# Triangular inverses of the gated delta rule: from six doubling levels on the matrix engine to 32x32 blocks solved by columns on the vector engine, with two levels left on the matrix engine

## The chip, the cores and the metric

The kernel runs on one core of a Trainium2 chip. The metric is the device time of one execution, in microseconds. Its engines are TensorE (PE in the profile; its weight loads are PEld), VectorE (DVE), ScalarE (ACT), GpSimd (POOL) and SyncE (SP, which only issues weight DMAs here).

## The reference, cut to what matters

Two transformer blocks on 256 tokens of width 2048: an attention block with a Fourier block, then a token mixer (a delta-rule part beside dilated attention) and a gated MLP. The change is in the delta-rule part of the token mixer, which has 8 heads of 128 and runs once forwards and once backwards over the tokens:

```python
def gated_delta_chunked(q, k, v, g, beta):
    ...
    cum_g = jnp.cumsum(g, axis=-1)
    gamma = jnp.exp(jnp.where(lower, cum_g[..., :, None] - cum_g[..., None, :], NEG_INF))
    k_beta = k * beta[..., None]
    a_mat = jnp.where(strict, jnp.einsum("bhnik,bhnjk->bhnij", k_beta, k) * gamma, 0.0)
    t_mat = a_mat + jnp.eye(c, dtype=jnp.float32)
    u = triangular_solve(t_mat, v * beta[..., None])
    w = triangular_solve(t_mat, k_beta * jnp.exp(cum_g)[..., None])
    qk = jnp.einsum("bhnik,bhnjk->bhnij", q, k) * gamma
    ...
    def step(state, xs):                      # over the chunks
        v_new = u_n - w_n @ state
        o_n = qd_n @ state + qk_n @ v_new
        state = state * dec_n + kt_n.T @ v_new
# q, k, v: silu of a depthwise convolution of width 5 over the projection n @ w_in; q, k normalized by head
o = delta(q, k, v, g_f, beta_f) + flip(delta(flip(q), flip(k), flip(v), flip(g_b), flip(beta_b)))
o = rms_norm(o) * silu(z)                     # then @ w_out, with the dilated half
```

## The kernel before, in words

The order of instructions on each engine is written out by hand. Weight matrices come in units of 128x2048 words (1 MB), which SP loads into four slots of `raw`. ACT copies a unit, rounded, into one of three `high` buffers (`act_hi`), DVE subtracts to get the rest (`dve_lo`), and PE runs three products a tile (high by high, high by low, low by high): 48 products of 128x256 a unit. ACT and DVE work two units ahead; `act_hi` of unit u waits until PE has used unit u - 3. Eight linears of four units make the inputs of the delta part: `("qkv", 0..5)` (q in 0 and 1, k in 2 and 3, v in 4 and 5) and `("z", 0..1)`. Beside them, as a `side` generator that is advanced once a unit, DVE runs the convolution (`dve_conv`, 24 tiles of 128x256, five operations each), and ACT the silu.

Then comes the delta part by itself (`pe_delta`, `dve_delta`, `act_delta`, end of `gpsimd_program`), and no linear runs beside it. The 256 tokens are two chunks of 128, so there are 16 matrices of 128x128 a direction (8 heads x 2 chunks), handled as 4 groups n of 4 matrices; one operation of 128x512 covers a group. In order: norms of q and k (`head_rstd`, `apply`), then for each direction `dr`: the decay matrices G from rows that PE spreads with a product by ones, A = beta * (k k^T) * G, the products k q, and the inverse of I + A by doubling. X starts as the inverse of 2x2 blocks, and level l = 1 to 6 joins pairs of blocks: POOL masks A by a constant (`L`), PE forms Y = L X, ACT copies Y, PE forms dXT and dX, DVE subtracts both. Then the scan over the two chunks (`vn` new values, `S` state, `kS`, `o` output), and after both directions the norm of the sum, the product with z, and its split into high and low. Only then does the next linear (`oM`, by `w_out`) start.

All products of the delta part are in plain float32; a product of 128 columns has two records in the trace, a transpose one.

## Time and profile before

| | us |
|---|---|
| median of 3 runs | 3241.22 (3228.16 to 3261.13) |
| the profiled execution, its time | 3227.28 |
| its span | 3225.5 |
| PE busy in the span | 3071.2 (95%) |
| DVE busy | 1855.3 (58%) |
| ACT busy | 1271.4 (39%) |
| POOL busy | 246.3 (8%) |

The first columns say what the whole takes. The page's 40 slices of the span (80.6 us each) show where: DMA falls from 192 GB/s to 33, 1 and 1 GB/s in slices 27 to 29, which is the delta part, where no weights are needed and the four slots are full.

### The profile page before, as it was taken

How to read it: one execution, taken by the hardware profiler on the slowest of the kernel's cores; microseconds unless marked ns; L12 is line 12 of the kernel's file. 1: busy time of each engine (PE TensorE's matmuls, PEld its weight loads, DVE VectorE, ACT ScalarE, POOL GpSimd, SP SyncE). 2: the span in 40 equal slices, each digit the busy share in tenths (PEclk: the TensorE clock that was granted, in tenths of full speed). 3: DMA queues.
4: the chain of work that ended last, by engine and by line, in shares of the span. 5: the costliest groups of instructions: out<-in, count | busy, mean ns of one | idle time of the engine just before them, and what ended most of it. 6: DMA issues, size and time to landing. Idle time of an engine off the chain costs nothing.

```text
span 3225.5 us, 52600 instructions
## 1 busy us (share of the span) xinstructions
PE 3071.2 (95%) x23262; PEld 2822.2 (87%) x23262; DVE 1855.3 (58%) x2132; ACT 1271.4 (39%) x1326; POOL 246.3 (8%) x244
## 2 busy tenths in 40 slices
PE   6999989988999999999999999998979999999998
PEld 3699775588988998989999989978879999999998
DVE  6746765466766434464544537755445667456653
ACT  7723331134433344343433425432233444344444
POOL 0001001000000000002112110032400000000000
PEclk8999999998999999989999989989989999999999
DMA  8746545354665553435444435500024555555553
GB/s 346 301 167 232 213 149 182 128 202 149 250 228 203 194 196 140 150 132 173 157 158 157 149 107 195 192 33 1 1 78 153 191 195 190 196 199 192 192 191 135
DMA packets 90850, 548.04 MB, mean 170 GB/s; under 512 B 10592, under 2 KB 10624, under 8 KB 45568
## 3 DMA queue, kind: packets, MB, share of 16 engines
q1 hardware_dynamic: 69408, 465.86, 40.4%
q0 software_dynamic: 18432, 67.12, 5.8%
q10 hardware_dynamic: 2784, 11.70, 0.9%
q8 instruction: 184, 3.01, 0.4%
q14 instruction: 42, 0.34, 0.0%
HBM read 542.54 MB, written 2.10 MB: 169 GB/s over the span
## 4 chain that ended last, share of the span: by engine, by line
PE 88%; DVE 5%; ACT 2%; issue 2%; DMA 1%; SPq 0%; DVEq 0%; ACTq 0%
PE bank L663 87%; DVE r L1812 2%; ACT r L1242 1%; DMA f<-in_units 1%; PE bank L725 1%; PE bank L994 0%; DVE f L1865 0%; DVE f L2351 0%; DVE f L2121 0%; ACT f L1359 0%; DVE f L1846 0%; DVE f L2240 0%; DMA f<-in_later 0%; DVE f L1988 0%; DVE f L2138 0%
## 5 line engine op out<-in xcount | busy, mean ns | idle before, releaser
L663 PE MATMUL bank<-r,r 128*128 128x256 f32 (+4 forms) x19360 | 2409.2, 287 | 62.3 <-DVE r L1812 31.3
L663 PEld LDWEIGHTS bank<-r,r 128*128 128x128 f32 (+3 forms) x19360 | 2297.4, 188 | 166.8 <-issue 76.3
L1812 DVE TENSOR_TENSOR r<-f,r 128x2048 fp32r<-128x2048 f32 (+2 forms) x466 | 1012.6, 2175 | 853.3 <-ACT r L1242 851.5
L1242 ACT CAST r<-f 128x2048 fp32r<-128x2048 f32 (+2 forms) x466 | 835.6, 1796 | 985.2 <-PE bank L663 803.3
L663 PE MATMUL bank<-f,f 128*128 128x128 f32 (+12 forms) x3390 | 639.4, 338 | 50.2 <-issue 7.3
L663 PEld LDWEIGHTS bank<-f,f 128*128 128x128 f32 (+6 forms) x3390 | 472.1, 196 | 161.5 <-issue 88.0
L1846 DVE SCALAR_TENSOR_TENSOR f<-f,f,f 128x512 f32<-128x512 f32 x240 | 180.0, 750 | 40.0 <-DMA f<-in_later 32.4
L2540 POOL DMA_DIRECT2D f<-in_later x128 | 67.8, 529 | 968.2 <-DVE f L1846 790.4
L1259 ACT COPY f<-bank 128x512 f32<-128x512 f32 (+2 forms) x141 | 80.2, 588 | 148.0 <-PE bank L663 142.5
L2289 DVE SCALAR_TENSOR_TENSOR f<-f,f,f 128x255 f32<-128x255 f32 (+1 forms) x272 | 131.7, 484 | 9.7
L2549 POOL TENSOR_TENSOR f<-f,f 32x512 f32<-32x512 f32 x24 | 30.9, 1289 | 735.5 <-PE bank L663 735.5
L725 PEld LDWEIGHTS bank<-f,f 128*128 128x128 f32 x288 | 37.4, 159 | 52.5 <-issue 20.3
L1408 ACT ACTIVATE f<-bank,f 128x512 f32<-128x512 f32 x32 | 22.0, 688 | 150.3 <-DVE f L1995 143.8
L2567 POOL TENSOR_TENSOR f<-f,f 128x512 f32<-128x512 f32 x56 | 72.2, 1313 | 52.3 <-PE bank L663 47.4
L2357 DVE TENSOR_TENSOR f<-f,bank 128x512 f32<-128x512 f32 x48 | 33.0, 688 | 69.2 <-PE bank L663 69.2
L725 PE MATMUL bank<-f,f 128*128 128x128 f32 x288 | 48.8, 310 | 25.1 <-ACT f L1408 10.1
L2552 POOL TENSOR_TENSOR f<-f,f 32x512 f32<-32x512 f32 x24 | 64.4, 2683 | 1.9
L1593 ACT COPY f<-bank 128x512 f32<-128x512 f32 x48 | 28.1, 586 | 87.5 <-PE bank L663 87.5
L1988 DVE TENSOR_REDUCE f<-bank 128x1 f32<-128x512 f32 x32 | 22.0, 689 | 57.2 <-PE bank L663 57.2
L1522 ACT ACTIVATE f<-f,f 128x768 f32<-128x768 f32 x16 | 15.0, 938 | 80.1 <-DVE f L2248 80.1
L2227 DVE TENSOR_TENSOR f<-bank,f 32x512 f32<-32x512 f32 x24 | 16.3, 679 | 45.4 <-PE bank L663 45.4
L1359 ACT ACTIVATE f<-f 128x256 f32<-128x256 f32 (+1 forms) x46 | 19.1, 433 | 50.8 <-PE bank L663 29.2
(205 smaller groups left out, 898.6 us busy)
## 6 DMA issues: line engine op xcount, KB each, us to landing
f<-in_units SPq DMA_DIRECT2D x346, 1024.0 KB, 4.8
f<-in_units SPq DMA_DIRECT2D x120, 768.0 KB, 4.3
f<-in_later POOLq DMA_DIRECT2D x128, 512.0 KB, 4.9
f<-in_units SPq DMA_DIRECT2D x8, 576.0 KB, 4.7
f<-in_x ACTq DMA_DIRECT2D x2, 1024.0 KB, 12.7
f<-in_ctx ACTq DMA_DIRECT2D x2, 1024.0 KB, 11.3
f<-in_x_turned ACTq DMA_DIRECT2D x1, 2048.0 KB, 11.1
f<-in_units SPq DMA_DIRECT2D x2, 800.0 KB, 4.4
```

Of the source, the lines that this page charges most:

```text
L663: return e.matmul(o, lhsT, rhs, start=start, stop=stop, skip_group_check=True)
L725: ins = e.transpose(o[:, j * 128:(j + 1) * 128], src(j), ident)
L1242: e.copy(unit_view(high[HIGH_OF[u]][1], u), unit_view(raw[RAW_OF[u]][0], u)).then_inc(*up("w_hi", ("hi", u)))
L1259: return e.copy(dst, src(ps("lin", name, q))).then_inc(*up("act_out", ("out", "lin", name, q), *names))
L1812: e.tensor_tensor(unit_view(raw[RAW_OF[u]][1], u), unit_view(raw[RAW_OF[u]][0], u), unit_view(high[HIGH_OF[u]][1], u).bitcast(F32), ALU.su ...
L1846: ins = e.scalar_tensor_tensor(o, w, s, o, ALU.mult, ALU.add)
L2289: ins = e.scalar_tensor_tensor(o[:, lo:hi], s[:, lo + d:hi + d], tap(j), o[:, lo:hi], ALU.mult, ALU.add)
L2357: e.tensor_tensor(gXT[:, n, :], gXT[:, n, :], ps("dXT", dr, l, n)[:, :], ALU.subtract).then_inc(*up("dve_delta", ("out", "dXT", dr, l, n), ...
L2540: e.dma_start(own[:, n % 2, :, :], a["later"][n // 8, n % 8].rearrange("p (k c) -> p k c", k=2)).then_inc(*up(f"own_half{n % 2}", ("own la ...
L2549: e.tensor_tensor(v, v, cos2.unsqueeze(1).to_broadcast([32, 2, T]), ALU.mult).then_inc(*up("pool_dil"))
L2552: e.tensor_tensor(v, v, two(rt[n % 2][0:32, :]), ALU.add).then_inc(*up("pool_dil", ("roped half", x, hf, br), ("half", n)))
L2567: e.tensor_tensor(v4(gL[:, m, :]), v4(gAT[:, m, :]), b4(ec[f"{lev}{l}"]), ALU.mult).then_inc(*up("pool_delta", ("L", dr, l, m)))
```

## The change

- The order of the linears is k, z, q, v (`MIXER`), and part of the delta work is run beside them: `pe_delta_ahead`, `act_delta_ahead` and `dve_delta_ahead`, each advanced once a unit (`under`). The 32 units of the eight linears are counted from 0 to 31 here; the numbers of `yield` set the unit.
- Ahead go the gates, the decay matrices of both directions (now Relu and Exp on ACT, from products that spread one column), the norm of k, k k^T (once for both directions), A (into `TT`, all 32 matrices), and the root of q's norm.
- DVE transposes the 32x32 diagonal blocks of A into `FF`, 32 matrices with four blocks each, and solves all 128 blocks at once by columns: 31 steps, each a product of a column by the rows solved so far and a subtraction, into `VB`. It needs `TT` at unit 18, and runs in units 19 to 24 of 32.
- After the linears `VB` is transposed into the diagonals of `VV` and `UU` (the inverses and their transposes), which lie where the linears' operand H was and are set to zero by POOL when the last two units are done.
- PE runs levels 5 and 6 alone. In level 6 and in half of level 5's products only 64 columns are computed.
- The products of k and q are shared by both directions, whose scans go side by side. Both directions add up in the same PSUM banks.
- Buffers of the delta part lie in the three `high` buffers, so the first units of `oM` are not split beforehand (`upto`). Unit 0 of `oM` is split once the last forward output exists, the others later.
- Five of the 24 convolution tiles are left for the delta part.

```diff
+MIXER = [("qkv", 2), ("qkv", 3), ("z", 0), ("z", 1), ("qkv", 0), ("qkv", 1), ("qkv", 4), ("qkv", 5)]
+TILES = [4 * b + i for name, b in MIXER if name == "qkv" for i in range(4)]
+CONV_RATE = [0, 0, 0, 0] + [1, 1, 1, 1] + [2, 2, 0, 0] + [0] * 12 + [2, 2, 1, 2] + [1, 1, 1, 1]
+GRP = [[(c, hf) for c in order for hf in range(2)] for order in ((0, 1), (1, 0))]
...
+def under(first, rates, second):
+    for n in rates:
+        run_on(first, n)
+        run_on(second)
+        yield
...
+        gL, gY = quads(high[0][0][:, :]), quads(high[1][0][:, :])
+        gG = [quads(high[2][0][:, :]), quads(flat3(TT)[:, 2048:4096])]
...
+            for dr in range(2):
+                for n in range(4):
+                    pe_gate_rows(e, SIDE, "G", dr, n)
+                    if n % 2 == 1:
+                        yield
+            for _ in range(5):
+                yield
+            for _ in pe_head_rstd(e, "dlk", 8, sqk):
+                pass
+            yield
+            yield
+            for p in range(4):
+                pe_apply(e, "dlk", 1, p, (2 * p, 2 * p + 1))
+                if p % 2 == 1:
+                    yield
+            for hf in range(2):
+                for c in range(2):
+                    pe_with_k(e, SIDE, "kk", c, hf, 8)
+                yield
+            for _ in range(13):
+                yield
+            for _ in pe_head_rstd(e, "dlq", 8, sqq):
+                pass
+            yield
...
+        def pe_delta(e):
+            four = range(4)
+            for n in four:
+                pe_gate_rows(e, ALLB, "Gq", 0, n)
+            for p in four:
+                pe_apply(e, "dlq", 0, p, (2 * p, 2 * p + 1))
+            for dr in range(2):
+                for n in four:
+                    pe_level_y(e, 5, dr, n)
+                for n in four:
+                    pe_level_5(e, dr, n)
+                if dr == 0:
+                    for n in (0, 1):
+                        pe_gate_rows(e, ALLB, "Gq", 1, n)
+                else:
+                    pe_turned_k(e, 0)
+                for n in four:
+                    pe_level_y(e, 6, dr, n)
+                for n in four:
+                    pe_level_6(e, dr, n)
+                if dr == 0:
+                    for n in (2, 3):
+                        pe_gate_rows(e, ALLB, "Gq", 1, n)
+            pe_turned_k(e, 1)
+            for c in range(2):
+                for hf in range(2):
+                    pe_with_k(e, ALLB, "kq", c, hf, 0)
...
+            for _ in range(17):
+                yield
+            e.wait_ge(*at("solved"))
+            e.wait_ge(*at("qkv", 7))
+            for _ in act_squares(e, "hrs", "dlq", [qkv[:, i, :] for i in range(8)], sqq, T):
+                pass
+            yield
+            act_head_root(e, "dlq", 0, 1.0)
+            yield
...
+        def act_delta(e, conv):
+            e.wait_ge(*at("used", LIN[MIXER[-1]].us[3]))
+            for n in range(4):
+                act_gate_rows(e, 0, n)
+            act_y(e, 5, 0)
+            act_y(e, 6, 0)
+            for n in range(4):
+                act_gate_rows(e, 1, n)
+            act_y(e, 5, 1)
+            act_y(e, 6, 1)
...
+            dve_head_rstd(e, "dlk", 1)
+            yield
+            for p in range(4):
+                dve_apply(e, "dlk", p, qkv[:, 8 + 2 * p:10 + 2 * p, :], 1.0)
+                if p % 2 == 1:
+                    yield
+            for hf in range(2):
+                for c in range(2):
+                    o = ps("kk", c, hf)
+                    e.wait_ge(*at("ps", "kk", c, hf))
+                    for dr in range(2):
+                        n = GRP[dr].index((c, hf))
+                        e.wait_ge(*at("exp G", dr, n))
+                        for j in range(4):
+                            v, x = mats(TT, dr, n)[:, j, :], 8 * dr + 4 * hf + j
+                            names = [("A", dr, n)] + ([("out", "kk", c, hf)] if dr else []) if j == 3 else []
+                            e.scalar_tensor_tensor(v, o[:, j * 128:(j + 1) * 128], bt[:, c, x:x + 1], v, ALU.mult, ALU.mult).then_inc(
+                                *up("dve_delta", *names))
+                yield
+            e.wait_ge(*now("dve_delta"))
+            for q in range(4):
+                qs_ = slice(32 * q, 32 * q + 32)
+                e.transpose(FF[qs_, :, :], TT[qs_, :, qs_].rearrange("p m a -> p a m")).then_inc(*up("dve_delta", ("F laid",)))
+            yield
+            e.wait_ge(*at("eye"))
+            for b in range(31):
+                k = 31 - b
+                t = tmpS[:, 0:k * (b + 1)].rearrange("p (a c) -> p a c", a=k)
+                w = VB[:, b + 1:32, 0:b + 1]
+                e.wait_ge(*now("dve_delta"))
+                e.tensor_tensor(t, FF[:, b + 1:32, b].unsqueeze(2).to_broadcast([128, k, b + 1]),
+                                VB[:, b, 0:b + 1].unsqueeze(1).to_broadcast([128, k, b + 1]), ALU.mult).then_inc(*up("dve_delta"))
+                e.wait_ge(*now("dve_delta"))
+                e.tensor_tensor(w, w, t, ALU.subtract).then_inc(*up("dve_delta", ("solved",)))
+                if b % 6 == 5 or b == 30:
+                    yield
+        def dve_turned_back(e):
+            e.wait_ge(*at("zero"))
+            e.wait_ge(*at("solved"))
+            for q in range(4):
+                qs_ = slice(32 * q, 32 * q + 32)
+                e.transpose(VV[qs_, :, qs_].rearrange("p m c -> p c m"), VB[qs_, :, :].rearrange("p a c -> p c a")).then_inc(
+                    *up("dve_delta", ("V laid",)))
+            yield
+            for q in range(4):
+                qs_ = slice(32 * q, 32 * q + 32)
+                e.transpose(UU[qs_, :, qs_].rearrange("p m a -> p a m"), VB[qs_, :, :]).then_inc(*up("dve_delta", ("U laid",)))
+            yield
...
+        def dve_delta(e, conv):
+            dve_head_rstd(e, "dlq", 0)
+            back = dve_turned_back(e)
+            run_on(back)
+            for p in range(4):
+                dve_apply(e, "dlq", p, qkv[:, 2 * p:2 * p + 2, :], B_SCALE)
+            run_on(back)
+            run_on(conv)
             for dr in range(2):
+                dve_qdec(e, dr)
+                dve_level_5(e, dr)
+                if dr == 1:
+                    dve_ktail(e, 0)
+                run_on(conv)
+                dve_level_6(e, dr)
+                run_on(conv)
+            dve_ktail(e, 1)
...
+            side = under(conv, CONV_RATE, dve_delta_ahead(e))
+            for name in MIXER:
+                dve_units(e, name, side, upto=first_unit(("oM", 0)) - 1)
+            dve_delta(e, conv)
...
+            us = LIN[MIXER[-1]].us
+            for u, m0, m1 in ((us[2], 0, 24), (us[3], 24, 32)):
+                e.wait_ge(*at("used", u))
+                e.memset(VV[:, m0:m1, :], 0.0).then_inc(*up("pool_delta"))
+                e.memset(UU[:, m0:m1, :], 0.0).then_inc(*up("pool_delta", ("zero",)))
             for dr in range(2):
+                for n in range(4):
+                    if dr == 1:
+                        e.wait_ge(*at("ps", "Y", 5, 0, n))
+                    e.wait_ge(*at("A", dr, n))
+                    e.tensor_tensor(v4(gL[:, n, :]), mats(TT, dr, n), b4(ec["pairs"]), ALU.mult).then_inc(*up("pool_delta", ("L", dr, n)))
+                e.wait_ge(*now("pool_delta"))
+                e.wait_ge(*at("F laid"))
+                e.memset(TT[:, 16 * (1 - dr):16 * (2 - dr), 0:64], 0.0).then_inc(*up("pool_delta", ("low zero", dr)))
```

What stands on DVE beside the linears, before (one unit of the convolution's stretch; L1812 is the subtraction of a unit, L2281 and L2289 the convolution of one tile):

```order
L1812 TENSOR_TENSOR r_2048_54<-f_2048_53,r_2048_58 128x2048
L2281 TENSOR_SCALAR f_6144_237<-f_2048_239,f_637_65 128x256
L2289 SCALAR_TENSOR_TENSOR f_6144_237<-f_2048_239,f_637_65,f_6144_237 128x254
L2289 SCALAR_TENSOR_TENSOR f_6144_237<-f_2048_239,f_637_65,f_6144_237 128x255 x2
L2289 SCALAR_TENSOR_TENSOR f_6144_237<-f_2048_239,f_637_65,f_6144_237 128x254
L1812 TENSOR_TENSOR r_2048_56<-f_2048_55,r_2048_62 128x2048
```

And after, units 16 to 19 (L1993 is the subtraction of a unit now, L2517 makes A, L2531 and L2534 are one column step of the solve):

```order
L1993 TENSOR_TENSOR r_2048_50<-f_2048_49,r_2048_58 128x2048
L2517 SCALAR_TENSOR_TENSOR f_4096_241<-bank,f_32_107,f_4096_241 128x128 x16
L1993 TENSOR_TENSOR r_2048_52<-f_2048_51,r_2048_60 128x2048
L2517 SCALAR_TENSOR_TENSOR f_4096_241<-bank,f_32_107,f_4096_241 128x128 x16
L1993 TENSOR_TENSOR r_2048_54<-f_2048_53,r_2048_62 128x2048
L2523 STREAM_TRANSPOSE f_1024_251<-f_4096_241 32x1024 x4
L1993 TENSOR_TENSOR r_2048_56<-f_2048_55,r_2048_58 128x2048
L2531 TENSOR_TENSOR f_256_253<-f_1024_251,f_1024_252 128x31
L2534 TENSOR_TENSOR f_1024_252<-f_1024_252,f_256_253 128x31
L2531 TENSOR_TENSOR f_256_253<-f_1024_251,f_1024_252 128x60
L2534 TENSOR_TENSOR f_1024_252<-f_1024_252,f_256_253 128x30x2
```

Work on A and the solve has moved in between the subtractions that PE's weights wait for. On PE, where the linears have ended, before (L725 transposes; f_2048_247 to 241 are A, L and X):

```order
L663 MATMUL bank<-f_768_91,f_1475_63 128x256 x16
L663 MATMUL bank<-f_32_105,f_2048_233 128x8
L725 MATMUL bank<-f_1475_63,f_6144_237 128x128 x16
L663 MATMUL bank<-f_2048_243,f_1475_63 128x512 x4
L663 MATMUL bank<-f_2048_249,f_1475_63 128x512 x4
L663 MATMUL bank<-f_6144_237 128x128 x32
L725 MATMUL bank<-f_1475_63,f_2048_245 128x128 x16
L663 MATMUL bank<-f_2048_241,f_2048_249 128x128 x16
L663 MATMUL bank<-f_2048_245,f_2048_243 128x128 x4
L663 MATMUL bank<-f_2048_243,f_2048_245 128x128 x4
```

and after (f_4096_117 is `VV`, f_4096_119 `UU`, f_2048_57 the masked A, f_2048_59 the copy of Y, f_4096_241 `TT`):

```order
L697 MATMUL bank<-f_384_233,f_32_105 128x128 x16
L697 MATMUL bank<-f_768_91,f_1475_63 128x256 x8
L697 MATMUL bank<-f_4096_117,f_2048_57 128x128 x16
L697 MATMUL bank<-f_2048_59,f_4096_119 128x64 x4
L697 MATMUL bank<-f_4096_119,f_2048_59 128x128 x4
L697 MATMUL bank<-f_384_233,f_32_105 128x128 x8
L697 MATMUL bank<-f_4096_117,f_4096_241 128x64 x16
L697 MATMUL bank<-f_4096_119,f_2048_59 64x64 x16
```

The six levels are gone from this place, and levels 5 and 6 of the forward direction follow the norm of q directly.

## Rows read from the trace of the kernel before

**Rows 1.** The page, part 4: who holds the chain that ended last, whole span.

```profile
PE 88%; DVE 5%; ACT 2%; issue 2%; DMA 1%; SPq 0%; DVEq 0%; ACTq 0%
```

**Rows 2.** Windows: from:to, length, busy (count) of each engine, PE clock, DMA share, GB/s.

```profile
1930.00:2104.40 174.40, 174.40 (x1530) 174.21 (x1528) 127.02 (x158) 80.48 (x79) 0.00 (x0) 0.99 0.55 193
2104.40:2155.10 50.70, 43.90 (x193) 29.66 (x193) 32.31 (x46) 18.25 (x36) 14.95 (x11) 0.83 0.06 21
2155.10:2215.90 60.80, 60.80 (x547) 60.80 (x546) 27.77 (x43) 14.65 (x25) 26.50 (x22) 1.00 0.01 1
2215.90:2267.40 51.50, 37.70 (x219) 31.35 (x217) 30.60 (x45) 11.10 (x19) 15.39 (x11) 0.86 0.00 0
2267.40:2329.40 62.00, 62.00 (x545) 62.00 (x545) 27.76 (x43) 14.62 (x25) 26.17 (x22) 0.98 0.01 1
2329.40:2359.00 29.60, 19.52 (x122) 17.92 (x120) 9.07 (x16) 3.51 (x6) 0.00 (x0) 0.83 0.00 1
2359.00:2379.60 20.60, 9.85 (x33) 5.00 (x33) 10.93 (x16) 11.26 (x19) 0.00 (x0) 0.74 0.00 0
2104.40:2379.60 275.20, 233.78 (x1650) 206.72 (x1649) 138.43 (x207) 73.39 (x130) 83.02 (x64) 0.90 0.01 5
```

**Rows 3.** Timeline of PE in the delta part: start, length, engine, line, operation, shape, count.

```profile
2118.71 11.22 PE L663 MATMUL bank<-f,f 8*128 8x256 f32 x36 [0.18 <-DVE f L1941]
...
2155.11 60.91 PE L663 MATMUL bank<-f,f 128*128 128x128 f32 x544
...
2241.98 10.92 PE L663 MATMUL bank<-f,f 128*128 128x128 f32 x32 [0.72 <-ACT f L1597]
...
2267.36 62.22 PE L663 MATMUL bank<-f,f 128*128 128x128 f32 x544
...
2367.55 5.73 PE L663 MATMUL bank<-f,f 8*128 8x256 f32 x16 [2.95 <-DVE f L1937]
```

**Rows 4.** The same view, small float32 products in an earlier stage.

```profile
705.49 1.84 PE L663 MATMUL bank<-f,f 128*128 128x4 f32 x16
```

**Rows 5.** Timeline of DVE beside the linears, same columns.

```profile
1953.25 0.18 DVE L2267 TENSOR_SCALAR f<-f 128x32 f32<-128x32 f32 x1 [2.16 <-ACT f L1550]
1953.46 0.19 DVE L2269 TENSOR_TENSOR f<-f,f 128x32 f32<-128x32 f32 x1
...
1957.66 2.29 DVE L1812 TENSOR_TENSOR r<-f,r 128x2048 fp32r<-128x2048 f32 x1 [2.20 <-ACT r L1242]
...
1960.25 2.04 DVE L2289 SCALAR_TENSOR_TENSOR f<-f,f,f 128x254 f32<-128x254 f32 x4
```

**Rows 6.** DVE's groups by shape, whole span: count | busy us, mean ns | idle.

```profile
L2357 DVE TENSOR_TENSOR f<-f,bank 128x512 f32<-128x512 f32 x48 | 33.0, 688 | 69.2 <-PE bank L663 69.2
...
L2351 DVE TENSOR_TENSOR f<-f,f 128x512 f32<-128x512 f32 x8 | 9.4, 1236 | 0.0
L1937 DVE RECIPROCAL f<-f 8x256 f32<-8x256 f32 x5 | 8.7, 1740 | 17.9 <-ACT f L1382 17.9
...
L2138 DVE SCALAR_TENSOR_TENSOR f<-f,f,bank 128x256 f32<-128x256 f32 x32 | 14.0, 476 | 2.0 <-PE bank L663 2.0
...
L1918 DVE TENSOR_TENSOR r<-f,r 128x1024 fp32r<-128x1024 f32 x4 | 4.9, 1220 | 0.0
```

**Rows 7.** POOL's groups, whole span.

```profile
L2567 POOL TENSOR_TENSOR f<-f,f 128x512 f32<-128x512 f32 x56 | 72.2, 1313 | 52.3 <-PE bank L663 47.4 <-DVE f L2346 3.6 <-DVE f L2351 1.3
...
L2609 POOL MEMSET const-float32-0.0<- 128x1 f32 x1 | 0.1, 98 | 0.2 <-issue 0.2
```

**Rows 8.** ACT's groups, whole span.

```profile
L1242 ACT CAST r<-f 128x2048 fp32r<-128x2048 f32 x342 | 653.1, 1911 | 760.0 <-PE bank L663 650.8 <-DMA f<-in_units 107.9 <-issue 1.2
...
L1583 ACT ACTIVATE f<-f 128x512 f32<-128x512 f32 x8 | 5.0, 626 | 5.0 <-DVE f L2333 5.0
...
L1539 ACT COPY f<-bank 128x256 f32<-128x256 f32 x8 | 3.0, 373 | 26.4 <-PE bank L663 26.4
```

More of the change, by code:

```diff
@@ L183, in plan @@
     add("ab", w, KT, [(4096, 32)], [(128, 32)] * 2)
-    for b in range(6):
-        add(("qkv", b), w, KT, [(512 * b, 512)], full * 4)
-    for b in range(2):
-        add(("z", b), w, KT, [(3072 + 512 * b, 512)], full * 4)
+    for name, b in MIXER:
+        add((name, b), w, KT, [((3072 if name == "z" else 0) + 512 * b, 512)], full * 4)
     for b in range(4):
@@ L2554, in gpsimd_program @@
                         n += 1
[L2555 to L2568 removed]
+            e.wait_ge(*at("ps", "dtv", 3, 1))
```

631 lines of the change are left out of this document (342 added, 289 removed).

## The prediction

> **What bounds the kernel now.** I read the chain that ended last first: PE holds 88% of it [rows 1], so time comes off only where PE works less or waits less. Then the 40 slices show a stretch without weight transfers, and windows cut it at the events of the timeline [rows 2]. The delta part, from the end of the linears (2104.4) to the first product of `oM` (2379.6), takes 275.2 us, all of it on the path. The reader is to see two kinds of row in it: the levels (60.8 and 62.0 us) with PE busy throughout at full clock, and the rest (50.7, 51.5, 29.6, 20.6) with PE waiting for ACT and DVE, at a granted clock of 0.74 to 0.86. The linears ahead of it (174.4 us for 32 units, 5.44 a unit) have PE full, but DVE busy for only 127.0 and ACT for 80.5. The change takes products from PE and puts work into that room on DVE.
>
> **Prices.** A float32 product of 128 columns costs 60.91 / 272 = 0.224 us [rows 3], at two of the 544 records a product; one by the norm's 256 columns 5.73 / 8 at a mixed clock, 0.45 at full clock (twice 0.224). Of 4 columns it costs 1.84 / 8 = 0.23 us, the same [rows 4]: the 64-column products save no PE time, and I price them at 0.224. The page "TensorE: Matmul & The Clock Gate" of the Trainium skill (Back-to-back issue gap) has an isolated gap of columns / 2.4 GHz + 2.5 ns; by it the 96 half-width products would cost half and the sum would be 10.7 us lower, against the row. A dependent small DVE operation follows the one before after 0.21 us with 32 elements [rows 5], and large ones grow by 1.04 ns an element (2.29 us for 2048, 1.22 for 1024) [rows 5, 6]: 0.2 us + 1.04 ns an element for a step that waits for the one before. A tile of convolution is 2.4 us.
>
> **Beside the linears, PE.** Added: sums of the gates 16 records (1.8), gate rows 32 products (7.2), k's norm 8 of 256 columns (3.6), its spreading 8 of 256 (3.6), k k^T 16 (3.6), q's norm 8 of 256 (3.6): 23.4 us, all on the path, as PE is full there.
>
> **Beside the linears, DVE.** The solve has 62 operations on sum (31-b)(b+1) = 5,456 elements, twice: 62 x 0.2 + 10,912 x 1.04 ns = 12.4 + 11.4 = 23.8 us. A from k k^T is 32 operations of 128 elements from PSUM, 0.33 us each (476 ns for 256 [rows 6], less 128 elements): 10.6. The norm of k takes 1.74 + 4 x 0.69. The four transposes into `FF` show in no row. From below they are bounded by 1024 contiguous elements, 1.22 us, from above by the slowest two-operand row, 1.236 us for 512 [rows 6], so 2.47; both sides of this operation hop in memory or work on strips, so I take the middle, 1.85, 7.4 for four. Off DVE go five tiles (12 us), moved behind the linears. In total 127 + 35 = 162 us of some 198: there is room on average. Locally there is not. Between units 16 and 27 DVE has 12 x 2.21 (subtractions) + 10.6 + 7.4 + 23.8 + 7 tiles (16.8) = 85.1 us, against PE's 12 x 5.44 + 1.8 = 67.1. It is 18 us behind; its lead is two units less the cast and subtraction (10.9 - 1.9 - 2.3 = 6.7 [rows 5, 8]) plus the k k^T beside it, 8.5. The remaining **10 us** are a wait of PE for the low part, in units 23 to 30. Bounds: with 1.22 a transpose 6 us; with 2.41 ns an element throughout (the 1236 ns row) 15 + 2.5 more, 27. Queued behind a late DVE are the convolution's tiles, then ACT's silu and next cast, which have slack of a unit.
>
> The page "Vector Engine (DVE) Microarchitecture Reference" of the Trainium skill (section 5.2) says that a stream which hops at each element costs 1.7 to 2.5 ns for a column in place of 1.05. By it a transpose would be 1.9 to 2.7 us, near or just over my upper end, and the rule speaks against this change; the solve's streams mostly run along rows and would keep the low price. No row of this trace hops, so it cannot say.
>
> **Behind the linears.** T is the end of unit 31.
> (a) To the point where `UU` is laid. POOL clears `VV` and `UU`: 3072 elements each after unit 30, 1024 each after 31. A clearing of one element shows 98 ns, a POOL product of 512 shows 1313, or 2.56 ns an element [rows 7]. It reads nothing, so I take 1 ns, near the 0.93 of ACT's casts [rows 8], which gives T + 3; at 2.56 it is T + 15. Behind that wait stand on DVE the `VV` transposes (7.4), four `apply` (2.8) and the `UU` transposes (7.4): **20.6 us**. PE has only 16 gate rows, 8 spreads and 16 products Y here, 10.8 us, hidden. Range 12.6 to 38.
> (b) From there to the end of level 6 backwards: 160 products (level 5 forwards 32, gate rows 16, Y and last of level 6 forwards 32, Y of level 5 backwards 16, and then 32 + 32), 35.8 us, and 8 transposes 1.0. PE waits for a bank that DVE frees after a convolution tile and a decayed q (2.9), for ACT's two gate groups ahead of its copies of Y (2.1: four Relu of some 0.27, two Exp of 0.6 each [rows 8]) and some 1 elsewhere: **43 us**.
> (c) Scan, both directions at once: DVE's k q products and right sides (1.4 + 8 x 0.61 + 4 x 0.61) end 10 us in, then 48 products (state, o, kS) 10.8, the last right side, new values and copy 3.7, 32 products 7.2: **32 us**. Its two counterparts before are 51.5 with the products ahead of the second direction in it, and 29.6 [rows 2].
> (d) From the last output to `oM`: 20.6 as before [rows 2] and 1.4 for copies: **22 us**. The split of `oM`'s first units hides in the norm and in unit 0.
> (e) Clock. The same 8-column and 8-row products that take 0.22 a record at full clock take 11.22 / 36 = 0.31, and 32 records take 10.92 in place of 3.6 where PE had been waiting [rows 3]. I add **8 us** for (b) and (c).
> Together 125.6 in place of 275.2.
>
> **The sum.** -275.2 + 125.6 + 23.4 + 10 = **-116 us**. The profiled execution's own time is 3227.3, of which 1.8 lies around its span; it becomes 3111. The median shown is 3241.2, 14 above it, and a median is what will be compared: **3125 us**. The rest of the kernel keeps its instructions.
>
> **The rivals.**
> - The vector engine's new work is slow (hops at 2.4 ns an element or more): 17 us more beside the linears, 8 in (a), about 3150. For it: no row shows such an access. Against: only the transposes hop at each element.
> - PE stays at the low clock: (b) and (c) hold 240 products, 54 us; with gaps at half clock they take up to 54 more, some of it inside waits. Rows of the delta part at 0.83 to 0.86 with a third of the time idle [rows 2] speak for about 35 more in all: 3155.
> - Cheaper than thought: transposes at 1.2, no clock loss in (b), PE's waits gone: 3095.
> - Slower than before: the solve paces the linears. 62 dependent operations lie between subtractions, and PE gets no weights while they run. From 0.38 us each (23.8 / 62) they would have to go to about 2.3 for the 116 us to be gone, 2.5 for 3250. The rows give 0.21 for small dependent ones [rows 5], tenfold less. A POOL that holds DVE up (the 1236 ns row stands beside POOL work) has nothing to do there.
> - The change doesn't move the work: the pieces ahead wait for each other and are still unfinished at T. `solved` is needed at unit 30 by q's norm and DVE would have caught up by then; a lag of 20 us would only shift time: 3145.
>
> **How the numbers follow.** Forecast 0.60 (3095 to 3150). Slow vector work 0.15, low clock 0.12, unfinished work 0.04, cheaper 0.07, slower 0.02. Leaving out half of the cheap and the far end of the dear cases, the range is **3085 to 3170**. A measurement of this kernel can tell about 1% (32 us, the spread of the three runs) from no change. All cases but the last are beyond it: faster 0.96, the same 0.02, slower 0.02.
>
> **What would show it.** The profile after should have the first product of `oM` some 116 us earlier; the linears at 205 to 210 us with PE's wait for the low part in units 23 to 30 and nowhere before; solve steps of 0.2 to 0.46 us; transposes between 1.2 and 2.5; a gap of PE after the first 16 Y products, ended by DVE's transposes and not by POOL; 64-column products at 0.22 each. The prediction is wrong if PE waits in units 2 to 15 for the gates or k's norm, if the clearing takes over 5 us, or if `oM`'s first four units run slower than 5.44 us by more than a few.

## The result

The changed kernel takes 3135.3 us (median of 4 runs, 3116.0 to 3144.6) against 3235.1 beside it: 0.967 of the kernel before, 95% interval 0.959 to 0.975. A later set of 6 runs gave 3119.5 us and 0.964 (0.959 to 0.968). The forecast was 3125, within 3085 to 3170. The profiled execution took 3116.0 us with a span of 3114.2; the forecast for it was 3111.

The chain that ended last (page, part 4), to be read beside [rows 1]: DVE has taken over a part of what PE held.

```profile
PE 84%; DVE 9%; ACT 3%; issue 3%; DMA 1%; POOL 0%; SPq 0%; ACTq 0%; DVEq 0%; POOLq 0%
```

The windows that answer to [rows 2], cut at the four steps of the prediction: the linears, then (a) until `UU` is laid, (b) to the end of level 6, (c) to the last output, (d) to `oM`, and the sum of these four.

```profile
1933.90:2152.00 218.10, 207.23 (x1698) 199.84 (x1698) 155.82 (x240) 104.84 (x139) 5.40 (x2) 0.97 0.45 155
2152.00:2175.00 23.00, 14.22 (x87) 12.42 (x85) 19.71 (x14) 11.98 (x29) 18.55 (x16) 0.78 0.14 46
2175.00:2216.00 41.00, 38.51 (x326) 37.64 (x326) 24.66 (x48) 15.63 (x40) 5.07 (x4) 0.92 0.00 1
2216.00:2250.00 34.00, 31.83 (x282) 31.32 (x281) 19.52 (x41) 9.80 (x16) 0.00 (x0) 1.00 0.00 1
2250.00:2271.00 21.00, 9.64 (x32) 4.83 (x33) 10.62 (x16) 14.36 (x23) 0.00 (x0) 0.76 0.00 1
2152.00:2271.00 119.00, 94.20 (x721) 86.20 (x720) 74.51 (x117) 51.77 (x107) 23.61 (x20) 0.89 0.03 10
```

The delta part went from 275.2 to 119.0 us, since PE has 721 records in it instead of 1650. The linears, counted here from the first product of `ab` (a small linear right ahead of unit 0, which the first window above leaves out) to the end of the last unit, went from 191.6 (1912.76 to 2104.4) to 236.0 (1916.05 to 2152.0). Net: -156.2 + 44.4 = -111.8 here, -111.3 in the spans. So less than a third of what the delta part lost came back in the linears; the question was which part of those 44.4 us is work, and which is waiting.

PE's timeline in the linears shows both: pieces of side work (`128x8`, `128*8`, `8*128`), and in brackets what it waited for. `L1993` is DVE's subtraction that makes a unit's low part, `L1486` ACT's squares of q.

```profile
1916.05 30.08 PE L697 MATMUL bank<-r,r 128*128 128x32 f32 x192
1949.10 2.44 PE L697 MATMUL bank<-f,f 128*128 128x8 f32 x16 [2.98 <-issue]
1951.39 8.39 PE L697 MATMUL bank<-r,r 128*128 128x256 f32 x48
1959.62 1.95 PE L697 MATMUL bank<-f,f 128*128 128x128 f32 x16
1961.32 5.90 PE L697 MATMUL bank<-r,r 128*128 128x256 f32 x48
...
2088.87 5.72 PE L697 MATMUL bank<-r,r 128*128 128x256 f32 x48 [0.39 <-DVE r L1993]
2096.43 12.91 PE L697 MATMUL bank<-r,r 128*128 128x256 f32 x96 [1.84 <-DVE r L1993]
2109.51 5.72 PE L697 MATMUL bank<-r,r 128*128 128x256 f32 x48 [0.17 <-DVE r L1993]
2116.72 5.72 PE L697 MATMUL bank<-r,r 128*128 128x256 f32 x48 [1.48 <-DVE r L1993]
2123.60 11.17 PE L697 MATMUL bank<-r,r 128*128 128x256 f32 x96 [1.16 <-DVE r L1993]
2135.03 5.73 PE L697 MATMUL bank<-r,r 128*128 128x256 f32 x48 [0.26 <-DVE r L1993]
2142.76 3.61 PE L697 MATMUL bank<-f,f 128*8 128x256 f32 x16 [2.00 <-ACT f L1486]
```

DVE's timeline at the end of the linears and in (a). The bracket of the first transpose is POOL's clearing; from there to 2174.31 DVE doesn't stop but for PE's last spreading product.

```profile
2139.43 0.35 DVE L2462 TENSOR_SCALAR f<-f,f 128x256 f32<-128x256 f32 x1
2139.81 2.04 DVE L2470 SCALAR_TENSOR_TENSOR f<-f,f,f 128x254 f32<-128x254 f32 x4
2141.77 1.84 DVE L2462 TENSOR_SCALAR f<-f,f 128x256 f32<-128x256 f32 x1
...
2153.97 8.91 DVE L2544 STREAM_TRANSPOSE f<-f 32x1024 f32<-32x1024 f32 x4 [3.89 <-POOL f L2811]
2162.91 1.88 DVE L2122 SCALAR_TENSOR_TENSOR f<-f,bank 128x512 f32<-128x512 f32 x3
2165.82 0.69 DVE L2122 SCALAR_TENSOR_TENSOR f<-f,bank 128x512 f32<-128x512 f32 x1 [1.03 <-PE bank L697]
2166.43 7.88 DVE L2549 STREAM_TRANSPOSE f<-f 32x1024 f32<-32x1024 f32 x4
```

### The profile page after: what moved, and what is told of

Its sections match the earlier page's. It is cut to its first block, busy times and chain, and to the rows that moved or that the text cites. A ratio compares the mean times of both kernels' runs of the same rounds, so it can differ in the third digit from the quotient of the medians.

```text
span 3114.2 us, 50912 instructions
## 1 busy us (share of the span) xinstructions
PE 2963.5 (95%) x22494; PEld 2725.6 (88%) x22494; DVE 1821.7 (58%) x2125; ACT 1273.2 (41%) x1361; POOL 193.5 (6%) x204
## 4 chain that ended last, share of the span: by engine, by line
PE 84%; DVE 9%; ACT 3%; issue 3%; DMA 1%; POOL 0%; SPq 0%; ACTq 0%; DVEq 0%; POOLq 0%
PE bank L697 83%; DVE r L1993 3%; ACT r L1369 1%; DMA f<-in_units 1%; PE bank L759 1%; DVE f L2470 1%; DVE f L2027 0%; PE bank L1028 0%; DVE f L2534 0%; DVE f L2531 0%; DVE f L2046 0%; DVE f L2544 0%; DVE f L2302 0%; DVE f L2523 0%; DVE f L2549 0%
## 5 line engine op out<-in xcount | busy, mean ns | idle before, releaser
L1993 DVE TENSOR_TENSOR r<-f,r 128x2048 fp32r<-128x2048 f32 (+2 forms) x466 | 1012.1, 2175 | 873.6 <-ACT r L1369 871.9
L697 PE MATMUL bank<-f,f 128*128 128x256 f32 (+16 forms) x2718 | 540.3, 344 | 48.3 <-DVE f L2122 7.6
L697 PEld LDWEIGHTS bank<-f,f 128*128 128x128 f32 (+6 forms) x2718 | 382.9, 191 | 150.0 <-issue 80.1
L759 PEld LDWEIGHTS bank<-f,f 128*128 128x128 f32 x256 | 30.5, 149 | 45.9 <-issue 21.4
L759 PE MATMUL bank<-f,f 128*128 128x128 f32 x256 | 40.1, 293 | 19.2 <-ACT f L1538 9.9
L2462 DVE TENSOR_SCALAR f<-f,f 128x256 f32<-128x256 f32 x112 | 41.5, 371 | 0.0
L1486 ACT ACTIVATE f<-f 128x256 f32<-128x256 f32 (+1 forms) x46 | 17.8, 429 | 43.2 <-PE bank L697 27.2
L2204 DVE SCALAR_TENSOR_TENSOR f<-bank,f,f 128x256 f32<-128x256 f32 x48 | 21.0, 480 | 18.7 <-PE bank L697 17.8
```

The source lines that it names most:

```text
L697: return e.matmul(o, lhsT, rhs, start=start, stop=stop, skip_group_check=True)
L759: ins = e.transpose(o[:, j * 128:(j + 1) * 128], src(j), ident)
L1993: e.tensor_tensor(unit_view(raw[RAW_OF[u]][1], u), unit_view(raw[RAW_OF[u]][0], u), unit_view(high[HIGH_OF[u]][1], u).bitcast(F32), ALU.su ...
L2462: ins = e.tensor_scalar(o, s, tap(r), None, ALU.mult)
```

## The experiments

The stages of every run, us, read from PE's timeline as above: linears; delta part; from the linears' end to the first product of level 5 that reads `UU` (in the joined2 to joined4 kernels it lies within a row); the sum of linears and delta part. Totals scatter by 0.3 to 1.4% from run to run, and outside of these stages, where no instruction differs, the profiled executions lie between 2754 and 2781 us. So what is worth 2 to 20 us is read from the stages of one profiled execution each. They scatter too: the two executions of the changed kernel differ by 2.5 us in the linears and 2.1 in the delta part. Part of that can be named: the first 192 records of the linears, ahead of everything that the experiments change, took 28.4 to 28.8 us in eight of the fourteen executions (28.5 in the kernel before) and 30.1 in the other six, the changed kernel's two among them. Differences of 3 us or less are therefore read from single rows here, and not from the stages.

| kernel | linears | delta | first product with `UU` | sum |
|---|---|---|---|---|
| before | 191.6 | 275.2 | | 466.8 |
| changed | 236.0 | 119.0 | 22.4 | 355.0 |
| changed, again | 238.5 | 116.9 | 22.4 | 355.5 |
| full_width | 236.3 | 119.5 | 22.4 | 355.8 |
| no_solve | 223.7 | 119.0 | 22.4 | 342.7 |
| more_solve | 249.5 | 119.0 | 22.4 | 368.5 |
| gates_later | 231.4 | 119.3 | 22.4 | 350.7 |
| serial | 198.4 | 207.1 | 108.0 | 405.5 |
| wide | 237.8 | 119.9 | 20.5 | 357.6 |
| q_first | 232.8 | 121.4 | 22.4 | 354.3 |
| joined | 229.2 | 122.3 | 20.5 | 351.4 |
| joined2 | 228.4 | 112.0 | | 340.4 |
| joined3 | 229.7 | 111.0 | | 340.8 |
| joined4 | 229.3 | 109.4 | | 338.6 |

**full_width: is a 64-column product cheaper?** The products of level 6 and the half products of level 5 are made 128 columns wide:

```
-ins = mm(e, o[:, j * 64:(j + 1) * 64], mats(TT, dr, n)[:, j, :], V4[:, j, 0:64], j == 0, True)
+ins = mm(e, o[:, j * 128:(j + 1) * 128], mats(TT, dr, n)[:, j, :], V4[:, j, :], j == 0, True)
```

> The 96 products of levels 5 and 6 that take 64 columns take 128 here (64 of them are not used afterwards); copies and subtractions keep their sizes. In the changed kernel one of their records takes 0.111 us (6.23 us for 56 of them), as a 128-column one does (0.11 us). Theory, that of the forecast: such a product costs the same at either width, and the stretch from the last laid U to the end of level 6, 41.8 us in the changed kernel, stays within 1.5 us of that. Rival: a product is paid by its columns; 64 more columns in each of 384 records at 2.4 GHz are 10.2 us, and the stretch takes 52 us.

Measured: from the first product with `UU` to the end of level 6 backwards, 40.6 us (2176.87 to 2217.45) against 41.7 (2174.41 to 2216.15), and 39.4 in the changed kernel's second execution. Twice the columns cost nothing that shows beside a scatter of 2 us, and the rival's 10 us are not there. (The 384 records of the expectation are 192 in the trace, two a product; half of 0.224 us for each of the 96 products gives the same 10 us.) PE's timeline of full_width; the like rows of the changed kernel are 14.32 us for 112 records and 0.68 for 8, and 6.23 for 56:

```profile
2180.26 14.05 PE L697 MATMUL bank<-f,f 128*128 128x128 f32 x120 [0.24 <-DVE f L2578]
2194.75 6.64 PE L697 MATMUL bank<-f,f 128*64 128x128 f32 x56 [0.44 <-ACT f L1698]
```

The formula of the Trainium skill that the prediction set against this (page "TensorE: Matmul & The Clock Gate", Back-to-back issue gap) is for a single isolated product; the same section says that a stream of weight loads and products is paced by both, and that the formula counts too little at few columns. By the formula alone this run would have been 10 us longer; the trace agrees with the other half of the section.

**no_solve, more_solve: does the solve pace the linears?** One leaves out all its steps but the last, the other makes each product twice:

```
 for b in range(31):
+    if b < 30:                # no_solve
+        if b % 6 == 5:
+            yield
+        continue
...
     e.tensor_tensor(t, ..., ALU.mult).then_inc(*up("dve_delta"))
     e.wait_ge(*now("dve_delta"))
+    e.tensor_tensor(t, ..., ALU.mult).then_inc(*up("dve_delta"))      # more_solve
+    e.wait_ge(*now("dve_delta"))
```

> Leaves out the steps of the solve of the 32x32 blocks except the last (60 of its 62 vector instructions), so that the inverses are not computed; all else stays. Theory: the 7.3 us that TensorE waits in the last ten units of the linears (5.3 us of it for VectorE's planes, 2.0 us for the squares of q) come from the vector queue being filled by the solve; without it the linears take some 229 us instead of 236, and the delta part stays at 119. Rival: the convolution tiles alone fill the queue; the waits stay, and the linears stay within 2 us of 236.

> Each of the 31 steps of the solve makes its product twice: 31 more dependent vector instructions of 0.20 to 0.43 us, some 10 us on VectorE, all in the last 14 units of the linears; the result is the same. Theory: the slack of VectorE is used up in these units, and 7 to 10 us of it become waits of TensorE: linears 243 to 246 us instead of 236. Rival: there is slack left (the waits stem from single late planes), and the linears stay below 239.

Measured: linears 223.7 and 249.5, that is -12.3 and +13.5 us. Without the solve PE runs 14 units in one row and waits for nothing in them:

```profile
2052.11 76.42 PE L697 MATMUL bank<-r,r 128*128 128x256 f32 x672
2128.58 3.61 PE L697 MATMUL bank<-f,f 128*8 128x256 f32 x16
```

The same 14 units and the wait behind them take 87.2 us in the changed kernel. 7.3 are the waits, 1.7 is the unit of 2096.43 at half clock, 1.7 the start of a row after a stop (5.72 for a lone unit, 5.46 within a row). That is 10.7 of the 12.3 us. The other 1.6 stand ahead of the solve, in the first 192 records (28.46 us here, 30.08 in the changed kernel), and are scatter. Both theories of the two expectations had the sign, and both were too small: I had counted the waits and not what follows them. In more_solve PE's timeline reads

```profile
2091.11 7.34 PE L697 MATMUL bank<-r,r 128*128 128x256 f32 x48 [3.79 <-DVE r L1993]
2101.41 7.32 PE L697 MATMUL bank<-r,r 128*128 128x256 f32 x48 [2.97 <-DVE r L1993]
2111.14 7.45 PE L697 MATMUL bank<-r,r 128*128 128x256 f32 x48 [2.40 <-DVE r L1993]
2118.97 5.92 PE L697 MATMUL bank<-r,r 128*128 128x256 f32 x48 [0.38 <-DVE r L1993]
```

The 31 added instructions hold DVE 10.7 us. They became 7.8 us of further waits and, net, 5 us of lower granted clock (0.77 over each of the three units of 7.3 to 7.5 us). DVE has no slack left there: another microsecond in the solve costs 1.3. Taking the solve away (21.2 us of DVE's time) gave back only 10.7, so about half of it does fit beside the linears.

**gates_later: the wait behind unit 1.** The prediction had named a wait for the gates in units 2 to 15 as a sign of error. One `yield` goes ahead of the sums in the queues of PE, ACT and DVE, and one fewer stands behind them:

```
 def pe_delta_ahead(e):
     yield
+    yield
     o = claim(e, SIDE, "cum")
...
-    for _ in range(5):
+    for _ in range(4):
         yield
     for _ in pe_head_rstd(e, "dlk", 8, sqk):
```

> The sums of the gates, and what hangs on them, stand one unit of the linears later in all queues; the norm of k and all after it stay where they were. Theory: TensorE's 2.98 us of waiting for the gates in the first units of the linears goes, and with it the one unit that ran at half clock behind it (8.39 us instead of 5.7): linears 230.5 us instead of 236. Rival 1: the half clock there has another cause, then only the wait goes: 233. Rival 2: the gates come later still, and the wait only moves one unit on: 236.

Measured: linears 231.4, -4.6 us. Wait and slow unit are both gone, 5.5 us together; rival 1 falls, since the 8.39 us unit became 5.90:

```profile
1947.39 1.85 PE L697 MATMUL bank<-f,f 128*128 128x8 f32 x16
1949.10 5.90 PE L697 MATMUL bank<-r,r 128*128 128x256 f32 x48
```

The stage agrees less well than it looks: 1.3 us came from the first 192 records (28.80 us), and 1.7 went again to a unit of 7.46 us behind the wait of 0.60 for k's norm, where the changed kernel had 5.72. The slow unit behind a short wait came back in this place in joined2, joined3 and joined4 (7.3 us each).

What the gates wait for is on ACT. From DVE's first operation (1944.93) to PE's first sum (1949.10) pass 4.2 us, and 2.6 of them are two loads of ACT's function tables in the changed kernel:

```profile
1945.72 1.28 ACT L1680 ACT_TABLE_LOAD   x1
1947.26 1.28 ACT L1681 ACT_TABLE_LOAD   x1
```

**serial: fewer products, or work taken under the linears?** The three generators of work ahead run after the last unit; PE's, and ACT's and DVE's likewise:

```
 side = pe_delta_ahead(e)
 for name in MIXER:
-    pe_linear(e, name, of_H, None, side)
+    pe_linear(e, name, of_H, None, None)
+run_on(side, 99)
 pe_delta(e)
```

> All that the changed kernel runs ahead under the linears (gates, decay matrices, norm of k, kk, A, the transposes, the solve) stands behind them here; the operations are the same ones. Theory: the change gains by two parts that add up: fewer products in the delta part, and work taken under the linears. The linears then take 192 to 194 us as before the change, the delta part 119 + 76 = 195 us (gates 5, sums 3, eight decay matrices 14, norm of k 9, A 9, transposes 8, solve 24, norm of q 6, less the 2 of clearing), so the kernel 33 us more than the changed one (25 to 45), some 3150 us: about 80 of the 111 us are then from the delta part's own work and 33 from the place. Rival: the place is what pays, since the products that went were replaced by chains of short operations with TensorE idle and at half clock; the delta part then takes 235 us or more, and the kernel comes within 35 us of the one before.

Measured: 3167.0 us (ratio 0.982, 0.976 to 0.988); linears 198.4, delta 207.1, sum 50.5 above the changed kernel. The rival (235 or more) falls; the theory's sum was 12 us short in the delta part, which ran at a mean clock of 0.67 up to level 5. PE's longest idle stretch is the solve:

```profile
2156.14 6.46 PE L697 MATMUL bank<-f 128*128 128x128 f32 x32
2198.39 12.24 PE L697 MATMUL bank<-f,f 128*8 128x256 f32 x60 [35.79 <-ACT f L1487]
```

So 61 of the 112 us come from the delta part's own operations and 51 from their place; I had expected 80 and 33. The linears took 6.7 us more than before without a wait or a lower clock in them; this is taken up at the end. The kernel before shows the same lower rate in a later stretch, so it need not come from the place of the work; without it the two parts are 68 and 44.

**wide, q_first, joined: three repairs.** wide makes one transpose of 128 partitions each for V and U, into a dense place and before the linears end, and copies from there:

```
+e.transpose(FF[:, :, :], VB[:, :, :].rearrange("p a c -> p c a"))
+e.transpose(UC[:, :, :], VB[:, :, :])
...
-    e.transpose(VV[qs_, :, qs_].rearrange("p m c -> p c m"), VB[qs_, :, :].rearrange("p a c -> p c a"))
+    e.tensor_copy(VV[qs_, :, qs_], FF[qs_, :, :].rearrange("p c m -> p m c"))
```

q_first changes the order of the linears and with it the places of the convolutions; joined is wide, q_first and gates_later together:

```
-MIXER = [("qkv", 2), ("qkv", 3), ("z", 0), ("z", 1), ("qkv", 0), ("qkv", 1), ("qkv", 4), ("qkv", 5)]
-CONV_RATE = [0, 0, 0, 0] + [1, 1, 1, 1] + [2, 2, 0, 0] + [0] * 12 + [2, 2, 1, 2] + [1, 1, 1, 1]
+MIXER = [("qkv", 2), ("qkv", 3), ("qkv", 0), ("qkv", 1), ("qkv", 4), ("z", 0), ("z", 1), ("qkv", 5)]
+CONV_RATE = [0, 0, 0, 0] + [1, 1, 1, 1] + [2, 2, 0, 0] + [1, 1, 1, 1] + [0] * 9 + [1, 1, 1] + [1, 1, 1, 1]
```

> The four transposes of 32 partitions by 1024 that lay V (8.91 us together) become one of 128 partitions by 1024 into a dense place, before the linears end, and four copies of 32x1024 into the cleared matrix; the same for U (7.88 us). Theory: a transpose is paid by the elements of a partition, so that one of 128 partitions takes 2.0 to 2.3 us as one of 32 does; with copies of 0.5 to 1.1 us U is laid 10 to 14 us after the linears' end instead of 22.3, and the delta part takes 107 to 111 us instead of 119; the linears grow by 0 to 4 us for the two transposes that they take in. Rival: a transpose is paid by its blocks, so that the two take 8 to 9 us each: the linears grow by 10 us or more and nothing is left of the gain.

> The linears run in the order k, q, first half of v, z, second half of v instead of k, z, q, v, so that the convolutions of four tiles of q (2.35 us each on VectorE) stand in units 12 to 15, where VectorE idles half of the time, and none beside the solve or right behind it; as many tiles as before are done when the linears end. Theory: the 7.3 us of waits in the last third, and the 1.7 us of half clock behind the longest of them, come from VectorE's whole load there; the linears take 228 to 230 us instead of 236. Rival: they come from the solve in its own units alone, where VectorE stays full; then the waits before 2110 us (2.2 us, and the 1.7 us of clock) stay, and the linears take 232 us.

> The gates one unit later, the wide transposes and the order k, q, half of v, z, rest of v, together. Theory: the three touch different places and add: linears 236 - 4.6 - 6 + 2 = 227 us, delta part 108 us, together some 20 us less than the changed kernel (3116 in its profiled run, so 3096). Rival: VectorE is full from A on, the two added transposes bring back waits of TensorE that the order took away, and only 13 to 15 us are gained.

Measured: wide gains nothing (delta 119.9). Its theory held for the transposes and failed for the copies. DVE's groups by shape in wide:

```profile
L2524 DVE STREAM_TRANSPOSE f<-f 32x1024 f32<-32x1024 f32 x4 | 8.2, 2052 | 0.1
L2555 DVE COPY f<-f 32x1024 f32<-32x1024 f32 x4 | 8.0, 1996 | 0.1
L2549 DVE COPY f<-f 32x1024 f32<-32x1024 f32 x4 | 7.6, 1911 | 3.0 <-POOL f L2816 2.9
L2539 DVE STREAM_TRANSPOSE f<-f 128x1024 f32<-128x1024 f32 x1 | 2.0, 2036 | 0.0
L2540 DVE STREAM_TRANSPOSE f<-f 128x1024 f32<-128x1024 f32 x1 | 1.2, 1217 | 0.0
```

A transpose of 128 partitions takes what one of 32 takes, and 1.22 us where both sides run along rows. The copies, priced at 0.5 to 1.1 us, took 1.9 to 2.0.
q_first took 3.2 us off the linears, not 7, and 1.6 of these are the first 192 records (28.43 us): the waits for `L1993` fell from 5.3 to 3.6 and the one for q's squares went, but its second convolution of q now stood ahead of the reciprocal for k's norm (wait 2.72 us in place of 0.60, then 3.54 us for 1.99 us of spreading). Both named cases are half right: the waits in the solve's own units stay, those behind it go. joined: linears 229.2, delta 122.3; 3115.6 us, ratio 0.966 (0.961 to 0.970), not told apart from the changed kernel. Of the 20 us that I expected 3.6 came: the linears missed by 2, and the delta part's 108 fell with wide's theory.

**joined2, joined3, joined4: why are the copies slow?** joined2 lets the transposes write in the order that the copies read, gives two of the eight copies to ACT, and clears the unit of the reciprocal:

```
-CONV_RATE = ... [2, 2, 0, 0] + [1, 1, 1, 1] + [0] * 9 + ...
+CONV_RATE = ... [2, 2, 0, 0] + [1, 0, 1, 2] + [0] * 9 + ...
-e.tensor_copy(VV[qs_, :, qs_], FF[qs_, :, :].rearrange("p c m -> p m c"))
+e.tensor_copy(VV[qs_, :, qs_], FF[qs_, :, :])
+for q in (2, 3):                                  # ACT
+    e.copy(UU[qs_, :, qs_], UC[qs_, :, :])
```

> As the joined kernel, with four differences: the two wide transposes write in the order in which the copies read (rows of 32 side by side, instead of single elements 32 apart); the copies of the last two quarters of U are ScalarE's; no convolution stands in the unit of the reciprocal for k's norm; one convolution tile moves from before the first inverse to within it. Theory: the copies cost 1.9 to 2.0 us each in the wide kernel because they read single elements 32 apart; read in rows they cost 0.5 to 1.1 us, V is laid some 6 us and U some 13 us after the linears' end, and the delta part takes 110 us instead of 119 to 122; the linears lose the 2.9 us of waiting for k's norm and the 1 us of half clock behind it, and take 225 to 227 us. Rival: the copies are slow because they write rows 128 apart, or because GpSimd works beside them; they stay at 1.9 us, U is laid 18 us or more after the linears' end, and the delta part stays at 118 us or more.

> The changed kernel itself, run beside joined2 on the same chip so that the two can be told apart from each other and not only from the kernel before: 0.967 of the kernel before, linears 236 us and delta part 119 us. What joined2 gains on it by either theory is 10 us (rival) or 18 to 20 us (theory), 0.3 or 0.6%.

Measured: 3103.4 us, ratio 0.961 (0.955 to 0.966), beside 3119.5 and 0.964 for the changed kernel; the intervals overlap, the stages do not: 340.4 against 355.5. The delta part fell to 112.0, near the theory. Yet a copy still took 1.60 us on DVE and 1.05 on ACT. `UU` was laid 14.3 us after the linears' end instead of 20.4, and most of that is work moved away: DVE's copies of V went from 7.7 to 6.4 us, those of U, two instead of four, from 8.1 to 3.3. joined3 writes the copies and the first tap in two-input forms; joined4 goes back to joined2 and holds POOL's products until V is laid:

```
-ins = e.tensor_scalar(o, s, tap(r), None, ALU.mult)                             # joined3
+ins = e.tensor_tensor(o, s, tap(r).to_broadcast([128, T]), ALU.mult)
-e.tensor_copy(VV[qs_, :, qs_], FF[qs_, :, :])                                   # joined3
+e.tensor_tensor(VV[qs_, :, qs_], FF[qs_, :, :], FF[qs_, :, :], ALU.max)
+e.wait_ge(*at("V laid"))                                                        # joined4, POOL
 for dr in range(2):
     for n in range(4):
```

> As joined2, but VectorE's six copies are made as TENSOR_TENSOR (maximum of a value with itself) instead of COPY, and the first tap of the convolutions of q, k and v as TENSOR_TENSOR with the tap broadcast instead of TENSOR_SCALAR; results and places are the same. Theory: while GpSimd clears or multiplies, it holds up VectorE's one-input forms (COPY 1.60 us where ScalarE takes 1.05 for as much; TENSOR_SCALAR 4.81 us beside the clearing, 0.35 alone), and not its two-input forms (2.04 us for four beside or without GpSimd). The first tap beside the clearing then takes 0.43 us, a copy 1.1 to 1.2 us, V is laid 2 us earlier, and the delta part takes 109 to 110 us instead of 112. Rival: the copies are slow by their strides, and a two-input form reads twice; a copy takes 1.6 us or more and the delta part stays at 112 or grows.

> As joined2, but GpSimd's first masked products wait until V is laid, so that it works beside VectorE's four copies of V only for the 0.95 us of clearing U. Theory: a copy of rows takes 1.60 us in joined2, and 1.96 as TENSOR_TENSOR in joined3, because GpSimd's products (1.24 us each alone, 1.68 and 2.04 there) and VectorE's instructions wait for each other; alone a copy takes 0.55 to 1.1 us, the four end 3.5 to 5.5 us after the linears instead of 7.5, the products take 1.24 us again, and the level starts as early as in joined2 or 1 to 2 us earlier: delta part 110 to 112 us. Rival: the copies are slow by the rows 128 apart that they write; they stay at 1.6 us each, GpSimd's products come 6 us later than now, and the delta part grows to 114 us or more.

Measured, the four copies of V on DVE and POOL's four products beside or behind them, in joined2, joined3 and joined4:

```profile
2140.97 6.42 DVE L2558 COPY f<-f 32x1024 f32<-32x1024 f32 x4 [1.05 <-POOL f L2825]
2141.80 6.72 POOL L2832 TENSOR_TENSOR f<-f,f 128x512 f32<-128x512 f32 x4
```

```profile
2144.23 7.84 DVE L2561 TENSOR_TENSOR f<-f 32x1024 f32<-32x1024 f32 x4 [4.43 <-POOL f L2828]
2145.06 8.15 POOL L2835 TENSOR_TENSOR f<-f,f 128x512 f32<-128x512 f32 x4
```

```profile
2148.09 3.55 DVE L2558 COPY f<-f 32x1024 f32<-32x1024 f32 x4 [1.06 <-POOL f L2825]
2151.72 4.96 POOL L2833 TENSOR_TENSOR f<-f,f 128x512 f32<-128x512 f32 x4 [2.77 <-DVE f L2558]
```

Apart, the two lots take 3.55 and 4.96 us; side by side in joined2, 6.42 and 6.72. They wait for each other, and the rows 128 apart that they write are not the cause: joined4's theory holds, and the rival of joined3 was right about its time and wrong about the cause. (Single elements 32 apart, as wide reads them, do cost: 2.00 us a copy beside the same products, 1.64 in rows.) What the edits reach bears it out better than the delta part as a whole: `UU` is complete 22.3 us after the linears' end in both executions of the changed kernel, 14.3 in joined2, 16.8 in joined3 and 12.3 in joined4.

The first of the four copies stands beside POOL's clearing of U and not beside its products. The shortest, median and longest of the four, in ns, for joined4 (COPY, then alone) and for joined3 (TENSOR_TENSOR, then beside the products):

```profile
L2558 DVE COPY f<-f x4: 683/687/1398, 2148.1 to 2151.0; 32x1024 f32<-32x1024 f32 x4
```

```profile
L2561 DVE TENSOR_TENSOR f<-f x4: 1215/2178/2179, 2144.2 to 2149.9; 32x1024 f32<-32x1024 f32 x4
```

So a COPY alone takes 0.69 us, and 1.40 beside the clearing; a TENSOR_TENSOR takes 1.22 beside the clearing, and 2.18 beside the products. joined3's theory is right for the clearing and wrong for the products, which hold up both forms. The first tap beside the clearing tells the forms apart too. joined4 has the one-input form, joined3 the other, both beside the clearing of 3072 elements (4.81 us spans two of them):

```profile
2138.50 4.81 DVE L2471 TENSOR_SCALAR f<-f,f 128x256 f32<-128x256 f32 x1
```

```profile
2135.08 0.42 DVE L2472 TENSOR_TENSOR f<-f,f 128x256 f32<-128x256 f32 x1
```

joined3: 3103.9 us, ratio 0.961 (0.959 to 0.962). joined4: 3101.0 us, ratio 0.959 (0.956 to 0.963), the lowest sum of stages, 16.4 us below the changed one. Neither the medians nor the sums (340.4, 340.8, 338.6) tell the three apart; that joined4 is the best of them rests on the 2.0 us by which its `UU` is complete earlier than joined2's.

## Why the prediction was right

The forecast of -116 us met -111.3, by steps that mostly held and two errors of 11 and 8 us that cancelled in part, which is luck.

- **Price of a product.** Right: 64 columns cost what 128 do (full_width).
- **Beside the linears, PE, +23.4.** Right. no_solve's linears are 32.1 us above those before; 3.6 of that are the waits for gates and reciprocal and 2.7 the slow unit, which leaves 25.8 for side work and for restarting a unit after each piece of it, 2.4 over the forecast.
- **Waits for the low part, +10, units 23 to 30.** The place was right: PE waits for `L1993` in units 23 to 30. 5.3 us are seen there as such, and 10.7 in all hang on the solve, with q's squares and what follows the waits. The lower bound given for this term, 6 us, should have been 7.5 by its own numbers (10 less four times 0.63). The solve's price was right too (23.8 forecast; 62 operations, 21.2 busy and some 2 of gaps).
- **The gates.** This is the step that failed: "nowhere before". Behind unit 1 PE waited 2.98 us, and the next unit took 2.7 us longer at a lower clock. The sums' queue place was one unit too early for a chain of eight small operations and two table loads between ACT and DVE, which I had counted as hidden and not laid out in time. That is 5.7 of the 11 us between +33.4 and +44.4. The others are 2.4 for side work, 1.6 for the start (30.08 us against 28.45 before, scatter), 0.7 for the solve and 0.6 for the wait for k's norm, which was a named sign of error too.
- **(a) 20.6.** 22.4. Clearing took 0.95 us for 1024 elements, as priced; a transpose 2.20 and 1.95 (2.05 for `FF`), and not 1.85. The low end given for this step, 12.6, left out the 3 us of clearing. Section 5.2 of the Trainium skill's "Vector Engine (DVE) Microarchitecture Reference" gives a stream that hops at each element 1.7 to 2.5 ns a column; the traces of these transposes agree with 1.9 to 2.2 ns, and with 1.2 where the stream runs along rows. Its verdict against the change was worth 2.0 us of DVE's time in (a) and 0.9 for `FF`.
- **(b) 43, (c) 32, (d) 22.** 41.8, 33.6, 21.3, one profiled execution each.
- **(e) Clock, 8.** Not there: (c) ran at 1.00 and (b) at 0.92, and their sum is 75.4 against 75 without the term.
- **The rivals.** Slow vector work did not come, and a low clock not in (b) and (c), where it was priced; (a) and (d) ran at 0.78 and 0.76, near the 0.83 and 0.74 of the like stretches before. "The solve paces the linears" came at its margin: not from 2.3 us an operation on, as I had written, but at once, 1.3 us for each further microsecond. What was missing for "slower" was size only. The unfinished work did not occur: DVE was through with the solve at 2114.5, 38 us ahead of T.
- **The median.** I had added 14 us from the profiled execution to the median, as it stood before. It was 19 here and -1 in the later set, so this term is scatter.

## What to carry to other kernels

Work put under a stretch that PE fills is paid at DVE's local load and not at its share of the whole: add up the queue unit by unit, and count with the waits of PE the clock that can follow them (1.6 to 1.7 us for a unit here, behind waits of 1.8 to 3.8; but the same wait of 1.84 us that was followed by a slow unit in the changed kernel was followed by one of 5.73 us in joined4). A chain of small operations across engines needs its length, table loads included, laid against the place of its consumer, even at the start where all engines look idle. And before work is handed to POOL, or copies put beside it, see what DVE has in those microseconds: one after the other the two were done in 8.6 us, side by side in 7.6, and the one that the path waits for took 6.42 instead of 3.55.
